# First modulation row turned on chip, small loads behind the first weights, causal mask added in the bank

## The reference

```python
def first_block(x, c, norm1_g, ...):
    cond = jax.nn.silu(c)
    for i in range(DEPTH):
        mod = cond @ ada_w[i] + ada_b[i]
        sh1, sc1, g1, sh2, sc2, g2 = jnp.split(mod[:, None, :], 6, axis=-1)
        h = rms_norm(x, norm1_g[i]) * (1.0 + sc1) + sh1
        ...
            y = diff_attention(h, diff_w_in[j], diff_w_out[j], ...)
        x = x + g1 * y
        h = rms_norm(x, norm2_g[i]) * (1.0 + sc2) + sh2
        y = hierarchical_moe(h, ...)
        x = x + g2 * y
    return rms_norm(x, final_norm_g)

def causal_attention_blocks(q, k, v, scale):      # 6 heads of 96, in the mixer
    ...
        s = jnp.einsum('bqhd,bkhd->bhqk', qblk, k).astype(jnp.float32) * scale
        s = jnp.where(allowed, s, -1e30)
        p = jax.nn.softmax(s, axis=-1).astype(v.dtype)
        return jnp.einsum('bhqk,bkhd->bqhd', p, v)
```

## Time and profile before

| | |
|---|---|
| median of 3 runs | 2575.57 us (2575.57 to 2578.04) |
| the profiled execution | 2573.11 us |
| its span, first to last instruction | 2571.2 us |
| PE busy | 2283.7 us, 89% |
| DVE busy | 1133.8 us, 44% |
| ACT busy | 612.3 us, 24% |
| mean granted TensorE clock | 0.952 |
| DMA | 586.95 MB, mean 228 GB/s |

### The profile page before, as it was taken

One profiled execution on the slowest core, in us unless ns is written; L12 is line 12 of the kernel. 1 busy time (PEld: TensorE's weight loads), 2 busy tenths in 40 slices (PEclk: granted clock), 3 DMA queues, 4 the chain that ended last, 5 costly groups with the idle time before them and its releaser, 6 DMA issues.

```text
span 2571.2 us, 35481 instructions
## 1 busy us (share of the span) xinstructions
PE 2283.7 (89%) x13340; PEld 1528.3 (59%) x13340; DVE 1133.8 (44%) x2034; ACT 612.3 (24%) x1246; POOL 303.1 (12%) x556
## 2 busy tenths in 40 slices
PE   4998896999989869999699998985998999998997
PEld 2874473565545448754456454544787767787765
DVE  2227756334334352392543333435338525227615
ACT  3114530000000032371100000003326215236213
POOL 0000101212122210000121222221001000001000
PEclk9998987999999979999799999997999799999799
DMA  6237947999999952204799999995221021211021
GB/s 250 98 129 298 343 171 283 419 418 419 416 420 368 420 209 98 101 3 175 296 419 419 419 415 419 372 419 191 98 71 50 1 114 44 94 60 66 1 82 42
DMA packets 129401, 586.95 MB, mean 228 GB/s; under 512 B 28420, under 2 KB 28454, under 8 KB 72570
## 3 DMA queue, kind: packets, MB, share of 16 engines
q1 hardware_dynamic: 114096, 566.15, 54.9%
q0 software_dynamic: 12096, 16.88, 1.8%
q10 hardware_dynamic: 3088, 2.27, 0.3%
HBM read 579.92 MB, written 27.31 MB: 236 GB/s over the span
## 4 chain that ended last, share of the span: by engine, by line
PE 72%; DMA 12%; DVE 10%; ACT 3%; issue 2%; POOL 1%; SPq 0%; DVEq 0%; ACTq 0%
PE banks L1358 15%; PE banks L1143 9%; PE banks L1144 9%; PE banks L1145 9%; PE banks L1376 8%; DMA normed_by_feature<-in_expert_w_up 6%; PE banks L1293 2%; PE banks L1171 2%; DVE normed_by_token L2313 2%; PE banks L1530 1%; PE banks L1339 1%; DMA weight_ring<-in_diff_w_in 1%; PE banks L1070 1%; DMA weight_ring<-in_sb_w_in 1%; PE banks L1386 1%
## 5 line engine op out<-in xcount | busy, mean ns | idle before, releaser
L1358 PE MATMUL banks<-weight_ring,scratch 128*64 128x256 f32 x3328 | 381.1, 383 | 28.5 <-DMA weight_ring<-in_expert_w_gate 14.2
L1358 PEld LDWEIGHTS banks<-weight_ring,scratch 128*64 128x64 f32 x3328 | 238.4, 138 | 190.3 <-issue 53.0
L1143 PE MATMUL banks<-weight_ring_rounded,scratch_rounded 128*128 128x512 f32 x768 | 304.1, 396 | 6.7 <-DVE ormed_by_feature_rounded L2159 4.7
L1145 PE MATMUL banks<-weight_ring_rounded,scratch_rounded 128*128 128x512 f32 x768 | 300.5, 391 | 0.0
L1144 PE MATMUL banks<-weight_ring_rounded,ormed_by_feature_rounded 128*128 128x512 f32 x768 | 300.5, 391 | 0.0
L2146 DVE TENSOR_TENSOR weight_ring_rounded<-weight_ring,weight_ring_rounded 128x4096 fp32r<-128x4096 f32 x27 | 119.5, 4424 | 232.0 <-ACT weight_ring_rounded L1631 232.0
L1143 PEld LDWEIGHTS banks<-weight_ring_rounded,scratch_rounded 128*128 128x128 f32 x768 | 145.1, 189 | 45.0 <-issue 9.0
L1145 PEld LDWEIGHTS banks<-weight_ring_rounded,scratch_rounded 128*128 128x128 f32 x768 | 145.1, 189 | 30.8
L1376 PE MATMUL banks<-normed_by_token,scratch 128*64 128x512 f32 x640 | 146.3, 599 | 18.5 <-ACT scratch L1842 18.5
L1144 PEld LDWEIGHTS banks<-weight_ring_rounded,ormed_by_feature_rounded 128*128 128x128 f32 x768 | 145.1, 189 | 28.7
L1840 ACT ACTIVATE scratch<-banks 128x256 f32<-128x256 f32 x72 | 27.7, 385 | 559.7 <-PE banks L1358 559.7
(11 more groups left out here) (384 smaller groups left out, 3447.2 us busy)
## 6 DMA issues: line engine op xcount, KB each, us to landing
weight_ring<-in_expert_w_gate SPq DMA_DIRECT2D x128, 1024.0 KB, 18.5
weight_ring<-in_expert_w_up SPq DMA_DIRECT2D x64, 1024.0 KB, 20.2
weight_ring<-in_expert_w_down SPq DMA_DIRECT2D x64, 1024.0 KB, 20.7
normed_by_feature<-in_expert_w_up SPq DMA_DIRECT2D x64, 1024.0 KB, 19.5
normed_by_token<-in_expert_w_down SPq DMA_DIRECT2D x64, 1024.0 KB, 20.0
weight_ring<-in_ada_w SPq DMA_DIRECT2D x20, 2048.0 KB, 11.8
weight_ring<-in_w_in SPq DMA_DIRECT2D x12, 2048.0 KB, 8.1
weight_ring<-in_diff_w_in SPq DMA_DIRECT2D x6, 2048.0 KB, 8.3
```

The lines of the kernel that those rows point to most:

```text
L1143: pe.matmul(out_ap, left_high, right_high, start=i == 0, stop=False)
L1145: last = pe.matmul(out_ap, left_high, right_low, start=False, stop=i == len(turn_order(stage)) - 1)
L1358: last = pe.matmul(PS[ROWS * half:ROWS * (half + 1), 1 + n // 2, 0:HIDDEN // 2], XGT[:, j, h, :], w[:, j, HIDDEN // 2 * half:HIDDEN // 2 * ...
```

## The change

- The four inputs become five. Only the first tables (identity, ones, the exponent -0.5, and a column that is 1 on partitions 64 to 127) are loaded at once; all other tables come with the late loads. The gain of the first norm comes as two rows, broadcast over partitions 64 to 127 of `FIRST_GAIN`, whose partitions 0 to 63 DVE sets to 1.
- The late loads (16 now, with the tables) are issued by SP ahead of the third unit of `qkv`, no longer by ACT at the start. The first unit of `qkv` is issued ahead of the fourth chunk of `ada_w`.
- DVE reads the modulation row out of its bank with one operation that adds the column and multiplies by `FIRST_GAIN`. PE turns it in four transposes into the same bank, DVE copies 32 values out as columns. The store to memory and the two loads go. PE turns block 7 after that. Blocks are now 128 features in a row, and the first projection's weights are loaded to match.
- ACT and DVE split the first unit in halves, before the modulation row.
- The preparation of lambda moves behind the last V block of `qkv`. PE waits for the late loads at the start of `diff`.
- In `latent` the mask's product on PE goes; DVE adds the mask to the last 128 columns in the bank. The scale is applied by ACT when it copies Q; DVE's product after the maximum goes.
- The counts of semaphores follow; the padding of the second attention signals on another one.

```diff
-            first = [(CCOL[:, 0, :], c[0]...), (X[:, :, :], x[0]...), (CON[:, :], tables),
-                     (GCOL[:, 0, :], norm1_g[0].rearrange("(p k) -> p k", p=P))]
+            first = [(CCOL[:, 0, :], c[0]...), (X[:, :, :], x[0]...), (CON[:, 0:EARLY_TABLES], tables[:, 0:EARLY_TABLES])]
+            first += [(FIRST_GAIN[HD + 32 * n:HD + 32 * (n + 1), :], norm1_g[0, BANK * n:BANK * (n + 1)].partition_broadcast(32)) for n in range(2)]
...
+            late = [
+                (CON[:, EARLY_TABLES:], tables[:, EARLY_TABLES:]),
...
+            def late_inputs():
+                    for dst, src in late:
+                        sp.dma_start(dst, src).then_inc(late_inputs_in, 16)
...
                     for i in range(MOD_CHUNKS):
+                        if i == MOD_CHUNKS - 1:
+                            qkv = stage_of("qkv", 0)
+                            width, k, src = whole_loads(qkv)[0]
+                            sp.dma_start(slot(qkv.load, width, k), src).then_inc(slot_loaded[qkv.load], 16)
+                            loaded_early.add(qkv.load)
                         sp.dma_start(FIRST_ADA[i], ada_rows(0, i)).then_inc(first_ada_in[i], 16)
...
                     if u == SLOTS:
-                        group_stored(sp, 0)
-                        modulation_columns(0, ((0, 0), (1, 1)))
+                        late_inputs()
...
@@ PE @@
                             fill_done(last, plan[0].fill)
+                            drained_wait(pe, plan[0].fill)
+                            for j in range(KD // 2):
+                                last = pe.transpose(bank(plan[0].fill)[:, j * P:(j + 1) * P], MOD_ROW[0][:, j * P:(j + 1) * P], ident)
+                            last.then_inc(first_columns_turned, 1)
+                            pe.wait_ge(dve_prepared, 2)
...
+                if stage.kind == "diff":
+                    pe.wait_ge(late_inputs_in, 16 * N_LATE)
...
-                                pe.matmul(bank(n)[:, 0:L], LQT(h)..., LKT(h)..., start=True, stop=False, ...)
-                                last = pe.matmul(bank(n)[:, L - P:L], ident, const("causal"), start=False, stop=True, ...)
+                                last = pe.matmul(bank(n)[:, 0:L], LQT(h)..., LKT(h)..., start=True, stop=True)
...
@@ ACT @@
-            with nc.allow_non_contiguous_dma(reason="a few positions"):
-                for dst, src in late:
-                    act.dma_start(dst, src).then_inc(late_inputs_in, 16)
...
+                    if stage.arg == ("first1", 0):
+                        u = product_after(stage).load
+                        loaded_wait(act, u)
+                        act.copy(rounded_slot(u + 1, BANK)[:, 0:KD // 2, :], slot(u, BANK)[:, 0:KD // 2, :]).then_inc(act_prepared, 1)
+                        act.copy(rounded_slot(u + 1, BANK)[:, KD // 2:, :], slot(u, BANK)[:, KD // 2:, :]).then_inc(slot_loaded[u + 1], 16)
...
-                            drained(act.copy(LQT(r // T)[0:MQ, :], bank(nq)[0:MQ, :]), nq)
+                            drained(act.mul(LQT(r // T)[0:MQ, :], bank(nq)[0:MQ, :], scale), nq)
...
@@ DVE @@
+            dve.memset(FIRST_GAIN[0:HD, :], 1.0)
...
-                        full_wait(dve, plan[0].fill)
-                        drained(dve.tensor_copy(MOD_ROW[0], bank(plan[0].fill)), plan[0].fill)
...
+                        (low halves of the first unit, two operations of 128x2048)
+                        n = plan[0].fill
+                        full_wait(dve, n)
+                        drained(dve.scalar_tensor_tensor(MOD_ROW[0], bank(n), const("second_half"), FIRST_GAIN, ALU.add, ALU.mult), n)
+                        dve.wait_ge(first_columns_turned, 1)
+                        by_chunk_of = bank(n).rearrange("p (j m c) -> p m j c", j=KD // 2, m=MOD_CHUNKS)[:, :, :, 0]
+                        dve.tensor_copy(COLS[:, 0:2, :].rearrange("p q (m j) -> p (q m) j", m=2), by_chunk_of).then_inc(dve_prepared, 1)
+                        dve.wait_ge(dve_prepared, 2)
...
-                        dve.wait_ge(mod_columns_in, 32)
-                        shift_and_gain(0, 0).then_inc(dve_prepared, 1)
...
-                            settle(dve.tensor_reduce(RCP[:, r % 4, 0:1], bank(n)[:, 0:L], AX, ALU.max, negate=True))
-                            dve.tensor_scalar(MX[:, r % 4, 0:1], RCP[:, r % 4, 0:1], scale_of(stage, r, scale), None, ALU.mult).then_inc(negmax_ready, 1)
+                            if stage.kind == "latent":
+                                diagonal = bank(n)[:, L - P:L]
+                                settle(dve.tensor_tensor(diagonal, diagonal, const("causal"), ALU.add))
+                                dve.tensor_reduce(MX[:, r % 4, 0:1], bank(n)[:, 0:L], AX, ALU.max, negate=True).then_inc(negmax_ready, 1)
...
@@ POOL @@
-                if stage.kind == "norm" and stage.arg == ("first1", 0):
-                    drained_wait(pool, plan[0].fill)
-                    store_group(0)
```

101 lines of the change are left out of this document (56 added, 45 removed).

## The result

The changed kernel takes 2564.52 us (median of 5 runs, 2557.43 to 2565.23); the kernel before, beside it, 2577.42 (5 runs, 2575.57 to 2578.52). The ratio is 0.995, with an interval of 0.9935 to 0.9965. The forecast was 2564.3.

A forecast was written before the change was run, and what follows sets the result against it. A chain of waiting stages on one core, three quarters PE, was taken to bound the kernel. Opening -8.4, seam +0.6 and latent -3.4 sum to -11.2, from the median 2575.6 to 2564.3 us; range 2557.5 to 2570.

The forecast's parts named there:

- Opening: Start up to the first scaling: inputs in at 10.3, scaling at 42.8 instead of 51.24, a gain of 8.4 us.
- Rival (a): Opening: the clock holds over PE's pause; gain 10.8 instead of 8.4, 2562.0 us in all; chance 0.12.
- Rival (d): Opening: held by loads, inputs at 12.7 and 1.5 more; gain 4.5, in all -7.3, 2568.3 us; chance 0.11.
- Rival (f): Opening: columns still wait for something else, such as first weights' split; only 2 or 3 us gained, 2573; chance 0.03.
- The rule on queues: Opening: the same bytes move whichever engine issues, so X stays at 12.4; gain 6.0 instead of 8.4.
- Seam: Between qkv and diff: moved lambda preparation delays DVE's first scores, +0.6 us lost in full; bounds 0.3 and 1.2.
- Latent: Two latent stages: mask on DVE and scale on ACT gain 1.7 a stage, 3.4 us for both.
- Rival (b): Latent stages: the mask's PE time comes back whole as DVE reorders its slack; -18.6 in all, 2557.0 us; chance 0.08.
- Rival (e): Latent stages: DVE's bank write far dearer than a read, addition 0.67; 5.2 us slower in all, 2581; chance 0.03.
- Rival (c): Latent stages: DVE is the bound outright, gain 0 there; in all -7.8, 2567.8 us; chance 0.13.
- The rule counted there: Latent stages: settling costs nothing extra, so they lose 0.4 instead of gaining 3.4; whole -7.4, 2568.2 us.

The follow-up runs named there:

- experiment 12: Changed kernel with convolution products on GpSimd, lambda preparation back in mid-qkv and block 6's four transposes made 13 times before the fourth chunk: 2557.13 us, ratio 0.9925.
- experiment 10: Changed kernel with the 16 late loads issued by ACT at its start again: 2574.02 us, ratio 0.9985 to the kernel before.
- experiment 9: Changed kernel with all constant tables loaded with the first inputs again, small loads still late on SP: 2566.25 us, ratio 0.9962 to the kernel before.
- experiment 3: Changed kernel with the preparation of lambda back in the middle of qkv, late loads still late: 2564.11 us, ratio 0.9937 to the kernel before.
- experiment 2: Kernel before with the latent change alone (mask added by DVE, scale in ACT's copy of Q): 2574.48 us, ratio 0.9988.
- experiment 5: Changed kernel with a discarded PE product of identity and mask ahead of each latent step's scores: 2568.49 us, ratio 0.9971 to the kernel before.
- experiment 4: Changed kernel with block 6's four transposes made six times between the third and fourth chunk, to fill PE's pause: 2566.1 us, ratio 0.9948.
- experiment 8: Changed kernel with the first projection's first weights loaded behind the fourth chunk of ada_w again: 2568.37 us, ratio 0.9971 to the kernel before.

## Why the prediction was right, point by point

**Opening: the steps right, the start of PE and two later terms too late.** Inputs in at 10.57 (10.3 said), chunks at 15.5, 20.5 and 25.5 and the weights at 30.9 (31.3), the fourth chunk at 35.9 (36.5), split of the weights done at 37.35 (37.5), hidden, the lower clock behind the pause, late loads landed by 47.65. What I had wrong is PE's start: 17.36, not 18.4. I let ACT's table load of 1.28 follow the inputs, as in the trace of before; with no issues ahead of it ACT makes it at 0.71 and it hides. That does not show at the scaling, since the loads set it by then. What does show came from the landing (0.6) and the small steps behind the chunk (0.4): the first scaling at 41.81, not 42.8, 9.4 instead of 8.4. Rival (a), the clock holding over the pause, did not happen, and experiment 12 prices it at 2.2 (2.4 said). Rival (d) did not happen. Rival (f) is refuted by the scaling's releaser, the columns, and by the split, which is done at 37.35, while PE ends the fourth chunk at 39.6.

**Which part of the opening carries the gain.** I had not separated them. The late loads off ACT's start: 9.4 by experiment 10, but with ACT held to 26.0. Held to 19.4, as in the kernel before, the turn on chip would give some 6.6 by the estimate there, and the loads off ACT the remaining 2.8. The tables' bytes 2.4; the first weights ahead of the fourth chunk 4.2, of which the instruction packet makes some 1.4. These don't add up, since each is read with the others in place.

**The rule on queues.** That X lands near 9.2 was right, and the reason given for it, the bytes that went elsewhere, was wrong. X landed at 9.2 in after; at 9.1 in experiment 9, with all tables behind it in the same queue; at 12.3 in the kernel before, with the same tables behind it and the 15 small loads on ACT's queue, 0.07 MB in 964 packets by then; and at 12.2 in experiment 10, with 1 MB of tables and the small loads on ACT's queue. So X comes 3 us earlier because the small loads left the other queue. How so few bytes hold it is not shown. The Trainium skill (DMA: Bandwidth & Descriptors, section "Issuing engines are not separate DMA queues") says that loads from different engines share the same DMA engines. The trace agrees in that loads issued by ACT delay one issued by SP. Its reading that leaves X where it was, since the same bytes move (a gain of 6.0 in the opening), is refuted. ACT's own time is a different thing: it was held for 26 us in experiment 10, by issuing.

**Seam: right.** +0.6 said, 0.67 measured, and experiment 3 shows that it is the lambda preparation.

**Latent: direction right, size off twice, and the two misses nearly cancel.** The terms: addition 0.28 said, 0.29 measured; settled start 0.32, measured 0.33. The mis-sized term is what DVE needs for a head. I took it from its 0.7 idle in 7.92, so 7.2, and came to 7.6. The stretch of that length in the kernel before has DVE busy for 6.92, so 1.0 idle: there was more slack than the idle column of one group says.

```profile
1967.44:1975.36 7.92, 7.44 (x56) 6.53 (x55) 6.92 (x22) 6.50 (x18) 0.00 (x0) 1.00 0.01 2
```

The after head takes 7.26 to 7.31 from copy to copy of Q. At full clock the stage gained 2.73 between the scores and 2.43 up to the next stage, not 1.7. Then the granted clock, on which I had no term for these stages: it stayed at 1.00 in both before, and fell in one of the two traced after, for a loss of 4.3 us; and again in the convolution behind the first stage, whose products took 1.7 longer. Over the traces a stage with the addition in the bank loses 4.1 to 5.6 in 5 cases of 14, some 1.6 a stage, and 1.7 behind it in 5 others, some 0.6 a stage. 2 x (2.43 - 1.6 - 0.6) is 0.5; the ratio of experiment 2 gives 3.1 (0.3 to 6.2); 3.4 was said. That the measured 3.1 is so near is luck: the interval holds the 0.5 as well, and in the traced execution of after the two stages with what follows them lost 1.1 in all.

Rival (b), PE's time back whole, is refuted by the head's 7.26 against PE's 6.72 of work. Rival (e), a dear write into a bank, by the 0.29. Rival (c), latent worth nothing, is refuted at full clock, by 40.87 against 43.61; in time, with the falls of the clock counted, it is hardly told from the 0.5. The rule counted there: the trace shows a price for settling, an operation that waits for one that settles starts 0.04 after its end, one that doesn't 0.08 before. The Trainium skill (VectorE: DVE Perf Modes, section "The DRAIN you can't avoid") says that a semaphore costs nothing extra; by that rule the stages would have lost 0.2 a head, and the measurement decides against it here.

**What stays open.** Why the clock falls in one latent stage and not in the next of the same code, and whether the pause of PE or its load makes a fall long. Experiment 5 rules out that PE's load alone prevents a fall. That the shorter pause prevents the long ones is likely (none in 12 stages with a pause under 2 us, 5 in 14 with one of 2.5) but not shown: no run changes the pause alone. The wander of unchanged stages is in part the clock. Between 196 and 300 us the shift of PE changes by -4.9 to +0.9 over the 13 traces and goes with the time at the lower level there (11.6 us less to 2.6 more than in before); the rest was not traced.

## What to carry to other kernels

Ask of every engine that issues loads at the start what it has to compute next: here 15 small loads held ACT's first operation to 19.4, though the inputs were in at 16.7, and they also held up the large input on the other queue by 3 us. Undo one part of such a change exactly, or the price read from it is another's: experiment 10 held ACT 6.6 us longer than the kernel before did.

Work that moves from the bound to an engine "with slack" changes the bound: after it, price the next 0.3 us on the receiving engine in full (an addition more a step made the kernel slower than before), and look for what that engine can hand on in turn, as the convolution products to GpSimd.

An engine's slack is read from its busy time in a stretch, not from the idle column of one group; and where TensorE's idle time grows in one place, put a price on its clock there, 4 to 6 us for each stage that is hit here and 1.7 in the stage behind, even though the trace of before shows none. And follow a gain up to the first operation of the next stage: 0.3 of the 2.7 between the scores did not get so far.

## What the runs showed of the hardware

- The clock can fall inside a dense stage: a pause of 2.5 us in a stage in which PE is busy for nine tenths went with 10 to 14 us at 1.2 GHz in 5 of 14 cases; with pauses under 2 us in 12 stages of other variants, none was so long.
- Useless work before a late load pays if it reaches the load: 5.9 us of repeated transposes saved 2.2 us behind it, 0.9 of which a later landing took; 2.8 us of them saved nothing.
- ACT loads its function table ahead of a wait when nothing else is ahead of it: at 0.71 instead of 19.42, 1.28 us off the path.
- One instruction packet of 16 KB, 1.1 us long on one DMA engine, goes with a 2 MB load that lands 1 us or more late: the fourth chunk comes 5.9 and 6.4 us behind the load ahead of it with the packet inside (experiments 4 and 12), the weights of experiment 8 in 6.9, and the chunk in 5.0 without it in seven traces. 15 of the 16 parts are in time, and one is late.
- Small loads on a second queue can hold a large one: X of 2 MB lands at 12.3 with 0.07 MB in 964 packets on ACT's queue beside it, and at 9.1 without them.
- GpSimd's product of 128x1024 takes 2.0 to 2.4 us to DVE's 1.22; DVE's additions beside it take 0.300 instead of 0.294.
